# Reordered VectorE, ScalarE and SyncE lists around the gated ConvFFN of a Griffin-style block, one core

## The reference

```
x = x + (g_a * branch_a + g_b * branch_b) @ w_out      # residual after the mixer
h = rms_norm(x, norm_ffn)
z = causal_dwconv(h @ w_up, conv_w, conv_b)            # w_up 1024 x 5632, width 3
val, gate = split(z)
x = x + (gelu(gate) * val) @ w_down                    # w_down 2816 x 1024
return rms_norm(x, norm_final)
```

## Time and profile before

| | us |
|---|---|
| median of 3 runs | 2679.16 (2678.57 to 2680.88) |
| profiled execution, its own time | 2677.93 |
| its span in the trace | 2676.1 |
| PE busy | 2531.0 (95%) |
| DVE busy | 1528.4 (57%) |
| POOL busy | 959.4 (36%) |
| ACT busy | 729.3 (27%) |
| mean granted TensorE clock | 0.98 of full |

### The profile page before, as it was taken

How to read it: one execution, slowest core, us unless ns; L and a number is a source line. 1 busy time by engine, 2 the same in 40 slices (tenths; PEclk the granted TensorE clock), 3 DMA queues, 4 the chain that set the end, 5 groups by cost and what they waited for, 6 DMA issues and landing times.

```text
span 2676.1 us, 34208 instructions
## 1 busy us (share of the span) xinstructions
PE 2531.0 (95%) x11906; PEld 2076.1 (78%) x11906; DVE 1528.4 (57%) x2209; ACT 729.3 (27%) x1413; POOL 959.4 (36%) x667
## 2 busy tenths in 40 slices
PE   4999999998999999797999999999989999999988
PEld 3787788886788888676878878888777888877877
DVE  7925355635788888426140235565458888883243
ACT  3125214212333333222121251142123333331111
POOL 1322222440233333474633222226103333336664
PEclk9999999998999999998999999999999999999999
DMA  5242342441122222544312123335211212125442
GB/s 182 94 102 85 134 142 95 142 173 55 57 85 84 80 86 94 212 162 141 133 55 94 53 99 136 117 111 177 109 48 72 93 73 91 76 89 212 141 173 102
DMA packets 117356, 298.53 MB, mean 112 GB/s; under 512 B 18136, under 2 KB 35320, under 8 KB 117256
## 3 DMA queue, kind: packets, MB, share of 16 engines
q1 hardware_dynamic: 78416, 217.22, 22.9%
q10 hardware_dynamic: 38840, 79.95, 8.5%
HBM read 228.45 MB, written 68.68 MB: 111 GB/s over the span
## 4 chain that ended last, share of the span: by engine, by line
PE 82%; DVE 11%; ACT 2%; DMA 2%; issue 2%; SPq 1%; POOL 0%; ACTq 0%; DVEq 0%; POOLq 0%
PE ps L414 25%; PE ps L416 25%; PE ps L415 25%; DMA act_hi<-ff 1%; DVE act_lo L1599 1%; DVE xres L1234 1%; PE ps L1940 1%; PE ps L1926 1%; DVE act_lo L1226 1%; PE ps L1875 1%; PE ps L1864 1%; PE ps L1791 1%; DVE slot_lo L1525 1%; PE ps L1943 1%; PE ps L1941 1%
## 5 line engine op out<-in xcount | busy, mean ns | idle before, releaser
L623 POOL CAST w_hi<-w_raw 128x1024 fp32r<-128x1024 f32 x72 | 78.7, 1093 | 747.9 <-PE ps L416 720.2
L666 POOL CAST slot_hi<-pair_raw 128x512 fp32r<-128x512 f32 x220 | 173.4, 792 | 478.7 <-PE ps L416 449.3
L414 PE MATMUL ps<-act_hi,w_hi 128*128 128x512 f32 x832 | 332.7, 400 | 8.6 <-DVE act_lo L1226 7.5
L416 PE MATMUL ps<-act_hi,w_lo 128*128 128x512 f32 x832 | 326.4, 392 | 0.0
L415 PE MATMUL ps<-act_lo,w_hi 128*128 128x512 f32 x832 | 325.6, 391 | 0.0
L414 PE MATMUL ps<-wd_hi,act_hi 128*128 128x512 f32 x704 | 278.9, 396 | 38.2 <-DVE act_lo L1599 38.2
L414 PE MATMUL ps<-act_hi,slot_hi 128*128 128x512 f32 x704 | 278.7, 396 | 14.8 <-DVE pre L1571 10.9
L415 PE MATMUL ps<-wd_lo,act_hi 128*128 128x512 f32 x704 | 277.6, 394 | 0.0
L415 PE MATMUL ps<-act_lo,slot_hi 128*128 128x512 f32 x704 | 277.3, 394 | 0.0
L416 PE MATMUL ps<-act_hi,slot_lo 128*128 128x512 f32 x704 | 277.2, 394 | 0.0
L416 PE MATMUL ps<-wd_hi,act_lo 128*128 128x512 f32 x704 | 276.9, 393 | 0.0
(11 more groups left out here) (319 smaller groups left out, 4903.8 us busy)
## 6 DMA issues: line engine op xcount, KB each, us to landing
w_raw<-in_wu SPq DMA_DIRECT2D x176, 512.0 KB, 3.4
pair_raw<-in_wu SPq DMA_DIRECT2D x88, 512.0 KB, 3.9
ff<-z SPq DMA_DIRECT2D x44, 512.0 KB, 2.6
act_hi<-ff SPq DMA_DIRECT2D x88, 256.0 KB, 3.6
gates<-junk ACTq DMA_DIRECT2D x64, 256.0 KB, 2.0
sig<-gates ACTq DMA_DIRECT2D x32, 512.0 KB, 5.2
tbl_o<-tables ACTq DMA_DIRECT2D x32, 384.0 KB, 3.4
tbl_r<-tables ACTq DMA_DIRECT2D x32, 256.0 KB, 2.7
```

The source lines that it names most:

```text
L414: nc.tensor.matmul(out, lh, rh, start=first, stop=False, skip_group_check=onto)
L416: return nc.tensor.matmul(out, ll, rh, start=False, stop=last, skip_group_check=onto)
L623: nc.gpsimd.tensor_copy(hi, w_raw[b][:, :]).then_inc(hi_made, 1)
L666: nc.gpsimd.tensor_copy(slot_hi[j][:, :, :], src).then_inc(slot_half[KIND[j]], 1)
```

## The change

Nothing that is computed changes. At the entry, in both blocks:

- `operand_low(0, 8)` on DVE and `operand_hi(0, 8)` on ACT go ahead of the scaling (DVE) and squares (ACT) of tiles 4 and 5.
- The scaled tile 7 goes to `x_last` (4 KB a partition at 164 KB, where `sums[0]` and `sums[1]` lie) instead of over `xres[7]`; the wait for the store of tile 7 stands ahead of `token_sum` step 2 of that tile, which writes `xres[7]`, and no longer ahead of its scaling.
- `slot_low` of S3 and S4 go ahead of the scaling of tile 7, those of W11 and W12 (period 1) between its token sums; S1's and S2's weight sums and S1's `slot_low` of period 1 move out of period 0 to between the operands.
- Operands 8 to 19 use a ring of four PSUM banks (2, 5, 6, 7).

At the end of the up phase c22 of period 21 goes ahead of `ff_mul` and of down_low, which are spread between c22, ff_mul and c12. On SP the store of the last product and the 4 or 8 MB of reloads go behind the loads of items 6 and 7. In the down phase `norm_x` of half 0 goes behind item 16 and half 1 behind item 18; `out_norm` is taken apart, with items 25, 26 and 27 ahead of the root, behind the second and behind the third scaling.

```diff
+        x_last = at("x_last", 164, [D])
         def operand_bank(m):
-            return 4 + m % 4 if m < KD else 5 + (m - KD) % 3
+            if m < KD:
+                return 4 + m % 4
+            return (2, 5, 6, 7)[m % 4] if m < 20 else 5 + (m - 20) % 3
...
+                for b in range(2):
+                    sp.wait_ge(ff_st[b], 16 * ((blk + 1) * (FT // 2) - 1))
                 store_ff(blk, 0, FT - 2)
                 load_down(blk, 0, 2, 0)
                 load_down(blk, 0, 3, 0)
-                store_ff(blk, 0, FT - 1)
-                for b in range(2):
-                    sp.wait_ge(ff_st[b], 16 * (blk + 1) * (FT // 2))
                 for k in range(4, 8):
                     load_down(blk, 0, k, 0)
                     load_ff(blk, 0, k, 0)
                     if k == 5:
+                        store_ff(blk, 0, FT - 1)
+                    if k == 7:
+                        for b in range(2):
+                            sp.wait_ge(ff_st[b], 16 * (blk + 1) * (FT // 2))
                         sp.wait_ge(x2_st, 16 * TT * (blk + 1))
...
                 ffn_root(0)
+                operand_hi(0, KD)
                 ffn_root(1)
-                operand_hi(0, KD)
...
-                with act.Fori(1, 5) as i:
+                with act.Fori(1, 4) as i:
                     for c in range(4):
                         down_hi(i, c)
-                if blk + 1 < BLOCKS:
-                    for h in range(2):
-                        x_squares(blk + 1, h)
-                        x_root(blk + 1, h)
-                for k in range(20, 23):
+                for k in range(16, 23):
                     down_hi(0, k)
+                    if blk + 1 < BLOCKS and k in (16, 18):
+                        x_squares(blk + 1, k // 2 - 8)
+                        x_root(blk + 1, k // 2 - 8)
...
                 down_hi(0, 24)
+                down_hi(0, 25)
                 root(stat_o, var_o, std_o, out_parts(blk), 0, 4)
-                for k in range(25, 28):
-                    down_hi(0, k)
+                down_hi(0, 26)
+                down_hi(0, 27)
...
+                def late(i):
+                    return xres[:, i, :] if i < TT - 1 else x_last[:, :]
...
-                    dve.wait_ge(x2_st, 16 * (blk * TT + hi))
+                    if hi < TT:
+                        dve.wait_ge(x2_st, 16 * (blk * TT + hi))
...
                 residual(4, 6)
+                operand_low(0, KD)
                 ffn_scaled(1)
-                operand_low(0, KD)
...
                 residual(7, 8)
-                ffn_scaled(3)
-                for t in range(4):
-                    token_sum(t, 3)
                 slot_low(S3, 0, 0)
                 slot_low(S4, 0, 0)
+                ffn_scaled(3)
+                token_sum(0, 3)
+                token_sum(1, 3)
+                slot_low(W11, 0, 1)
+                token_sum(2, 3)
+                token_sum(3, 3)
+                slot_low(W12, 0, 1)
+                operand_low(8, 12)
                 slot_low(W22, 0, 0)
-                slot_low(W11, 0, 1)
-                slot_low(W12, 0, 1)
                 conv_row(0, 0)
-                for m in range(8, OPERANDS, 4):
-                    operand_low(m, m + 4)
+                operand_low(12, 16)
+                operand_low(16, 20)
+                weight_sum(S1, 0, 1)
+                operand_low(20, 24)
+                slot_low(S1, 0, 1)
+                weight_sum(S2, 0, 1)
+                operand_low(24, 28)
...
                     c11(i, c)
                     if not end:
                         slot_low(S2, i, c + 1)
+                    else:
+                        c22(i, c)
+                        down_low(0, 0)
+                        down_low(0, 1)
                     if not first:
                         ff_mul(i, c - 1)
...
                     c12(i, c)
                     if not end:
                         slot_low(S4, i, c + 1)
+                    else:
+                        down_low(0, 2)
+                        down_low(0, 3)
...
-                with dve.Fori(1, 5) as i:
+                with dve.Fori(1, 4) as i:
                     for c in range(4):
                         down_low(i, c)
-                if blk + 1 < BLOCKS:
-                    for h in range(2):
-                        norm_x(blk + 1, h)
-                for k in range(20, 23):
+                for k in range(16, 23):
                     down_low(0, k)
+                    if blk + 1 < BLOCKS and k in (16, 18):
+                        norm_x(blk + 1, k // 2 - 8)
...
                 down_low(0, 24)
-                out_norm(blk, 0, 4, out_parts(blk))
-                for k in range(25, 28):
-                    down_low(0, k)
+                down_low(0, 25)
+                out_root(blk, 0, 4, out_parts(blk))
+                out_scaled(0)
+                out_scaled(1)
+                down_low(0, 26)
+                out_scaled(2)
+                down_low(0, 27)
+                out_scaled(3)
```

More of the change, by code:

```diff
@@ L1227, in transposed_lo, with out_root @@
                         ALU.mult, ALU.subtract).then_inc(act_ready, 1)
-            def out_norm(blk, lo, hi, part):
+            def out_root(blk, lo, hi, part):
                 norm_scale(stat_o, lo, hi, sq_o, blk * TT + hi, var_o, std_o, part)
@@ L1232, in out_norm, with out_scaled @@
                     dve.wait_ge(gfin_in, 16 * (blk + 1))
+            def out_scaled(i):
+                stt(xres[:, i, :], xres[:, i, :], stat_o["rstd"][:, i:i + 1], gfin[:, :], ALU.mult, ALU.mult).then_inc(o_ready, 1)
+            def out_norm(blk, lo, hi, part):
+                out_root(blk, lo, hi, part)
                 for i in range(lo, hi):
-                    stt(xres[:, i, :], xres[:, i, :], stat_o["rstd"][:, i:i + 1], gfin[:, :], ALU.mult, ALU.mult).then_inc(o_ready, 1)
+                    out_scaled(i)
             def norm_x(blk, h):
@@ L1531, in ffn_scaled @@
                         dve.wait_ge(gffn_in, 16 * (blk + 1))
-                    dve.wait_ge(x2_st, 16 * (blk * TT + hi))
+                    if hi < TT:
+                        dve.wait_ge(x2_st, 16 * (blk * TT + hi))
                     for i in range(lo, hi):
-                        stt(xres[:, i, :], xres[:, i, :], stat_f["rstd"][:, i:i + 1], gffn[:, :], ALU.mult, ALU.mult).then_inc(xf_ready, 1)
+                        stt(late(i), xres[:, i, :], stat_f["rstd"][:, i:i + 1], gffn[:, :], ALU.mult, ALU.mult).then_inc(xf_ready, 1)
                 def token_sum(t, i):
-                    early, late = xres[:, i, :], xres[:, HK + i, :]
+                    early, high = xres[:, i, :], late(HK + i)
                     if t == 0:
@@ L1541, in token_sum @@
                         dve.wait_ge(ftr_done, blk * OPERANDS + KD)
-                        ins = tt(early[:, 0:HALF], late[:, 0:HALF], early[:, 0:HALF], ALU.subtract)
+                        ins = tt(early[:, 0:HALF], high[:, 0:HALF], early[:, 0:HALF], ALU.subtract)
                     elif t == 1:
                         dve.wait_ge(tok_ready, blk * 16 + token_no(0, i))
-                        ins = tt(t2tok[:, i, :], late[:, HALF:], early[:, 0:HALF], ALU.subtract)
+                        ins = tt(t2tok[:, i, :], high[:, HALF:], early[:, 0:HALF], ALU.subtract)
                     elif t == 2:
-                        ins = tt(late[:, 0:HALF], late[:, HALF:], late[:, 0:HALF], ALU.subtract)
+                        if i == HK - 1:
+                            dve.wait_ge(x2_st, 16 * TT * (blk + 1))
+                        ins = tt(xres[:, HK + i, 0:HALF], high[:, HALF:], high[:, 0:HALF], ALU.subtract)
                     else:
@@ L1652, in period @@
                         slot_low(W22, i, c)
-                    if not end:
+                    if not end and not first:
                         weight_sum(S1, i, c + 1)
@@ L1672, in period @@
                         slot_low(W12, i, c + 2)
-                    if end:
-                        for k in range(4):
-                            down_low(0, k)
-                    if not first:
+                    if not first and not end:
                         c22(i, c)
@@ L1784, in operands @@
                     if m >= 4:
-                        pe.wait_ge(f_act, blk * OPERANDS + (m - 3 if m < KD else m - 2))
+                        pe.wait_ge(f_act, blk * OPERANDS + (m - 3 if m < 20 else m - 2))
                     for q in range(4):
@@ L1788, in operands @@
                         c2 = slice(HALF + k * P, HALF + (k + 1) * P)
-                        src = (xres[:, q, c], xres[:, q, c2], xres[:, q, c], t2tok[:, q, c], xres[:, HK + q, c2],
+                        src = (xres[:, q, c], xres[:, q, c2], xres[:, q, c], t2tok[:, q, c],
+                               xres[:, HK + q, c2] if q < HK - 1 else x_last[:, c2],
                                xres[:, HK + q, c], xres[:, q, c2])[kind]
@@ L2062, in _ @@
                 operands(blk, 16, 20)
```

(3 more changed lines are left out.)

## The result

The changed kernel takes 2587.57 us (median of four runs, 2586.11 to 2588.69) against 2679.26 (also of four), ratio 0.9657, 95% interval 0.964 to 0.9673. That is 91.7 us less where I had forecast 79; the time lies 0.6 us inside the fast edge of the range of 2587 to 2619, and outside the 2590 to 2608 that I had given the forecast itself.

The account below looks back on a forecast made before the run. PE was taken as the bound, full in the steady up phase, so only its idle stretches could pay. Terms 36 + 15 + 10.4 + 17.4 = 79 us gave 2600 us, range 2587 to 2619 (forecast's own 2590 to 2608).

Parts of the forecast that it names:

- Entry, operands 4 to 7: Entry of the up phase: making operands' low parts ahead of tiles 4 and 5 gains 6.2 us a block.
- Entry, operands 8 to 15: Up-phase entry: x_last, fourth PSUM bank and shorter DVE list save 2.8 + 2.8 us idle plus clock, 8.6 together.
- First periods: Entry's first periods: c12 comes about 4 us earlier, so PE's waits of 1.95 and 1.20 go, 3.1 us.
- End of the up phase: c22 and items 6 and 7 go earlier; the stall returns at item 8; gains 7.8 (block 0) and 7.1 us.
- the 11 to 15 that I had named as the sign: Block 0, before item 8: one long wait of PE, 11 to 15 us, expected if the forecast holds.
- the 27 us from reload to weight: End of the up phase, block 0: some 27 us from the start of the reloads to item 8's weight.
- Next block's norm: Down phase, block 0 only: splitting the normalization removes the 7.61 us wait and 2.8 of clock, 10.4 us.
- Output scaling: Down phase, items 25 to 28: splitting the four scalings removes waits of 7.94 and 7.84 us; 17.4 us booked.
- the port shared with POOL: Rival, down phase: DVE waiting out POOL's subtractions uses up the slack, costing 5 to 15 us; 2605 to 2615; chance 0.14.
- the reloads are only moved: Rival: POOL's splits run later, reloads start later, the end of the up phase gives nothing; 2615 us; chance 0.08.
- Half the entry: Rival: DVE or tile 7's store is late for operand 8, the 8.6 us stay in both blocks; 2617; chance 0.04.
- no gain at all: Rival, loop of periods: DVE meets POOL's casts worse and becomes the bound, eating all 79 us; chance 0.01.

Follow-up runs that it names:

- e6: The changed kernel with tile 7 scaled in place again, behind the wait for its store: 2598.98 us, 11.4 more than the changed kernel.
- e7: The changed kernel with the ring of three PSUM banks for operands 8 to 19 again: 2601.93 us, 14.4 more than the changed kernel.
- e9: The changed kernel with operands 0 to 7 behind the squares and scaling of tiles 4 and 5 again: 2602.86 us, 15.3 more.
- e3: The kernel before with only the next block's normalization moved behind items 16 and 18: 2669.39 us, ratio 0.9961, 10.3 less.
- e2: The kernel before with only the end of the up phase changed (c22 first, reloads behind items 6 and 7): 2660.6 us, 19.1 less.
- e5: The changed kernel with SP's old order (last product's store and reloads ahead of items 6 and 7), c22 still early: 2598.16 us, 10.6 more.
- e10: The changed kernel with the last period's c22 behind the gate product and four low parts again, SP's new order kept: 2596.05 us, 8.5 more.
- e1: The kernel before with only the entry's edits (x_last, the ring, DVE's and ACT's lists up to operand 27): 2639.12 us, ratio 0.9847, 40.5 less.
- e8: The changed kernel with reloads of 1 MB issued one behind each of items 7 to 14, next block's x first: 2574.24 us, 13.3 less.

## Why the prediction was right, and where its terms were short

The direction and every named mechanism held; the sum of 79 us was 12.7 us short of the measured 91.7 (10.2 short of the traces' 89.2), nearly every term erring to the same side. That the time still lies inside the stated range, by 0.6 us, is luck: 1 us more of gain in any term would have left it. The terms:

- **Entry, operands 4 to 7** (6.2 a block): 6.5 and 7.5. I took block 1 as equal to block 0, and it was not: matmuls behind its wait of 5.53 us stayed at the lower clock, and where block 0 waits 2.79 us before operand 11, block 1 waited 3.67.
- **Entry, operands 8 to 15** (8.6): 9.3 and 10.0. I had left out the wait of half a microsecond before each later operand group; with four banks two of the four went, 1.1 us. e6 and e7 show that `x_last` and the fourth bank are each needed, and e9 that the first reordering is worth 14 to 15 us alone. The slack of 1 us behind the store's new wait was enough: DVE has no idle time before that sum (643.82).
- **First periods** (3.1): 3.8. c12 came 5.41 us after c22 (672.54 - 667.13) where it had come 9.28 after (691.72 - 682.44), the 4 us I had. No run isolates this term.
- **End of the up phase** (7.8 and 7.1): 10.0 and 7.6. That the stall of 13.37 returns two items later was right, though its 10.64 lies just under the 11 to 15 that I had named as the sign; the 27 us from reload to weight were right too. The step that failed in size is when the reloads start: I had them 33.5 us after p7, they started after 31.8 (1091.17 - 1059.39), because the gate product ended 0.9 later and not 1.8 (7.95 us behind p7 against 7.07), and POOL took 4.7 us and not 5.2 for items 2 and 3.
- **Next block's norm** (10.4): 11.3 by distance, 10.3 alone in e3 (10.6 in its trace). Of the 11.3, 0.7 belongs to the term above: 9 matmuls behind item 8's wait ran at the lower clock, where 12 had behind item 6's.
- **Output scaling** (17.4): 19.7 by distance, 20.8 alone. The 1 us of waiting a block that I had booked as thin slack turned out as 0.25 and none.

Idle time and clock were both short: my terms hold about 59 us of waits and 19.5 of clock, the page shows 65.7 and 23.5.

Of the rivals, the port shared with POOL is real but did not use up the slack: in the root even operations over 128 x 4 took over 2 us, and single scalings 3.4, yet item 28 was only 0.25 us late. The rival that the reloads are only moved, with no gain from this stage, did not occur: e2 gained 19.1 us. The part of it that was in the forecast itself, a stall that comes back two items later, did. Half the entry and no gain at all did not occur; the steady up phase is filled by PE as before.

## What to carry to other kernels

Where one engine is full in the steady phase, list its waits one by one and move in its helper's list whatever is due next ahead of whatever is merely ready; each wait of 3 us and more was worth its length plus 1 to 3 us of low clock, unless a later wait took the gain back, as item 8's did with c22's in block 0. Apply the parts one at a time to the kernel before: here the four added up to within 1 us, so each could be judged alone. A bulk transfer in the queue of the just-in-time loads is best cut up between them: putting it two items later gained 4 us in block 0 (e5), cutting it into single megabytes gained 13 us more.

## What the runs showed of the hardware

- The granted clock fell behind every wait of PE of 2.9 us and more in the up and down phases of these runs, though not always at once. Behind the 4.07 us at 1069.53 in e10 the first matmul already takes 0.80 us. Behind the 4.06 us at 2340.20, before the same product in block 1, the first two run at the full clock and the drop comes with the third:

```profile
2340.20 0.50 PE L417 MATMUL ps<-act_hi,slot_hi 128*128 128x512 f32 x1 [4.06 <-DVE pre L1590]
2340.54 0.39 PE L418 MATMUL ps<-act_lo,slot_hi 128*128 128x512 f32 x1
2340.77 0.55 PE L419 MATMUL ps<-act_hi,slot_lo 128*128 128x512 f32 x1
2341.12 0.63 PE L417 MATMUL ps<-act_hi,slot_hi 128*128 128x512 f32 x1
```

  So a first matmul of 0.50 us does not show that the clock stayed full. The 3.04 us at 2409.71 in e1 and the 2.91 at 648.13 in e7 are of the same kind. Where a product's matmul ended the wait, some 7 to 14 matmuls behind it ran at the lower level and took 1.6 to 3.0 us more than at the full clock; waits of 4.06 and 4.07 us alone cost from 1.7 to 3.0. Behind waits of 0.9 to 2.2 us in these phases there was no drop.
- Small operations wait for POOL as long as large ones. In the changed kernel the root's operations over 128 x 4 take 0.16 to 0.18 us where nothing is in the way; two of them took 2.36 and 2.25, and each ended just behind a subtraction of POOL:

```profile
1207.40 2.36 DVE L1217 TENSOR_SCALAR var_out<-ssq_out 128x4 f32<-128x4 f32 x1
...
1211.43 2.25 DVE L1224 TENSOR_SCALAR nt_out<-nt_out 128x4 f32<-128x4 f32 x1
```

```profile
1207.01 2.72 POOL L631 TENSOR_TENSOR wd_lo<-w_raw,wd_hi 128x1024 fp32r<-128x1024 f32 x1
...
1211.27 2.39 POOL L631 TENSOR_TENSOR wd_lo<-w_raw,wd_hi 128x1024 fp32r<-128x1024 f32 x1
```

- The changed kernel, e1, e5, e7, e8 and e10 are the same up to operand 4's transposes, and reach them at 611.36 to 613.16 us. A difference of 2 us in such a start says nothing of the edit; distances between instructions do. Long ones have a spread too: from the first `down_add` of block 0's pass 1 to tile 5's residual in block 1, which no edit touches, the thirteen traces show 568.2 to 569.9 us.
